# Weighing the values in pairs of units, up to two units behind the transposes, in a two-block attention kernel

## The chip, the cores and the metric

The kernel runs on one core of one Trainium2 chip. The metric is the device time of one execution in microseconds; the time given is the median of several executions.

## What is computed

Two blocks run one after the other on x of 2048 rows by 1024 columns, float32. The first has a gated short convolution and a "stick-breaking" attention. The second, in which the change lies, makes a projection of 2888 columns, a pooling mixer, and a sparse attention: an indexer of 8 heads scores all keys, the best 256 keys of each query are selected, and 8 heads (64 wide, 2 groups of keys and values) attend to the selected keys alone. Cut to what matters:

```python
def one_block(blk, qb, qib, wb):              # a block is 128 queries
    q_pos = blk * Q_BLOCK + jnp.arange(Q_BLOCK)
    logits = einsum('bqhd,bsd->bqhs', qib, k_idx) * IDX_DIM ** -0.5
    score = einsum('bqhs,bqh->bqs', relu(logits), wb) * N_IDX_HEADS ** -0.5
    score = where(key_pos[None, :] <= q_pos[:, None], score, -inf)
    _, sel = top_k(score, 256)
    s = einsum('bqhgd,bqkhd->bqhgk', qg, k[sel]) * HEAD_DIM ** -0.5
    p = softmax(where(sel <= q_pos, s, -inf))
    return einsum('bqhgk,bqkhd->bqhgd', p, v[sel])
```

The kernel does not gather. It computes the attention scores against all keys that are causal for the block, adds a bias of -1e30 to those that were not selected, and sums over all.

## The kernel before, in words

`phase_select_attend` is written as one program per engine, which meet at semaphores. The 16 blocks of 128 queries are taken in the order `ORDER` = 0, 1, 4, 6, 8, 10, 12, 14, 15, 13, 11, 9, 7, 5, 3, 2. Block number b of the sequence has `keys(b)` = 128 x (ORDER[b] + 1) keys, in groups of up to 512 (`parts`): 1, 1, 2, 2, 3, 3, 4, 4, 4, 4, 3, 3, 2, 2, 1 and 1 groups. A **slot** is a pair of heads ("sides" 0 and 1) of a block, four slots a block; a **unit** is one group of keys of one slot. There are 64 slots and 160 units, and as each block has four slots, every block begins with an even unit.

All engines walk over the units in step. For unit u:

- TensorE transposes the unit's exponentials of both sides (`turn_over`, L3167 to L3175; up to 4 transposes of 128 by 128 a side) into one of two PSUM banks `turn`, which it may only overwrite when ScalarE has copied the last contents out. It then makes the products of `share(u)` (`scores`, L3127 to L3154): products of the indexer for a block three ahead, and attention products for a slot some 1.6 slots ahead, each as two matmuls of up to 512 columns into one of five banks `pr`. Last it weighs (`weigh`, L3177 to L3190): per 128 keys and side one product of the probabilities with the values, 128 keys by 64 columns, added up in the single PSUM bank `o_ps` of the block. It is issued one unit behind. The trace records each such product as two matmuls, so a full unit has 16 records of L3188. In L3182 the first weighing of a block waits until ScalarE has copied `o_ps` of the block before.
- ScalarE copies the transposed exponentials of both sides to SBUF (`leave`, L2777), applies ReLU to the indexer's products (`rectify`, L2769), and computes the exponential of a whole row when its last attention product is masked (`raise_e`, L2760; up to 2048 wide). Then come the rarer steps: the copy of `o_ps` (`leave_outputs`, L2785), a sample, a square and four counts for the selection of the block two ahead.
- VectorE adds the bias to the attention products and finds their least value (`mask`, L2902), adds up the index scores (`add_score`, L2890), searches the threshold, and divides the copied outputs (`divide`, L3047).
- GpSimd does small steps of the search; SyncE loads queries, keys, values and the output weights and stores the outputs.

The work of a share is spread evenly by time (`timed`, L2432 to L2440). Probabilities have three buffers (`P_DEEP` = 3, L2383): `leave(u)` waits for the weighing of unit u - 3. `leave_outputs(qb - 1)` waits for the last weighing of block qb - 1. In the kernel before it stands at the end of the first unit of block qb in ScalarE's order:

```python
                qb = block_of(u)
                if first_step(u, 0) and qb:
                    leave_outputs(qb - 1)
```

and TensorE's order is, from L3192:

```python
            for u in range(-1, U):
                if u >= 0:
                    turn_over(u, 0)
                    turn_over(u, 1)
                for kind, qb, h, m in share(u):
                    scores(kind, qb, h, m)
                ...
                if u >= 1:
                    weigh(u - 1)
            weigh(U - 1)
```

Of the kernel before, what the change touches and what calls it, by code (L numbers as in the profile page):

```python
# [2358 lines left out]
def phase_select_attend(nc, sem, p_t, rot_hi, rot_lo, bit_int, bit_val, half_powers, rank_row, inverse_t, mix_t, ident, space, w_out):  # L2359
# [37 lines left out]
    def parts(qb):  # L2397
        return [(at, min(GROUP, keys(qb) - at)) for at in range(0, keys(qb), GROUP)]
# [5 lines left out]
    def groups_of(s):  # L2404
        return parts(s // PAIRS)
# [27 lines left out]
    for s in range(SLOTS):  # L2433
        qb, pair = divmod(s, PAIRS)
# [10 lines left out]
    U = len(units)  # L2445

    def share(u):

        if u < 0:
            return [p for at, p in timed if at < 0]  # L2450
        s, g = units[u]
        steps = len(groups_of(s))
        return [p for at, p in timed if at >= 0 and int(at) == s and int((at - s) * steps) == g]
# [18 lines left out]
    def first_step(u, pair):  # L2472
        return units[u][0] % PAIRS == pair and units[u][1] == 0

    def block_of(u):
        return units[u][0] // PAIRS
# [8 lines left out]
    def values_due(u, chunk):  # L2485

        return first_step(u, 1) and block_of(u) == max(0, first_with(chunk) - 2)
# [16 lines left out]
    with ExitStack() as ctx:  # L2504
# [252 lines left out]
        def _(act):  # L2757
            nc.scalar.preload_act_table_set("natural_log_exp_and_others")

            def raise_e(qb, h):  # L2760
                s, side = qb * PAIRS + h // 2, h % 2
                act.wait_ge(masked, masks[qb, h, len(parts(qb)) - 1] + 1)
                if qb >= 2:
                    act.wait_ge(inverted, qb - 1)
                row = arg[:, s % DEEP, side, 0:keys(qb)]
                nc.scalar.activation(row, row, ACT.Exp, scale=-1.0, bias=low_top[:, s % DEEP, side, len(parts(qb)) - 1:len(parts(qb))],  # L2766
                                     accum_out=total[:, qb % 2, h:h + 1]).then_inc(raised, 1)

            def rectify(qb, h, m):  # L2769
                n, half = parts(qb)[m][1], m % 2 * GROUP  # L2770
                p, a = number["index", qb, h, m], adds[qb, h, m // 2]
                act.wait_ge(product, p + 1)
                if a >= R_DEEP:
                    act.wait_ge(scored, a - R_DEEP + 1)
                nc.scalar.activation(relu[:, a % R_DEEP, half:half + n], pr[p % BANKS][:, 0:n], ACT.Relu).then_inc(relu_done, 1)  # L2775

            def leave(u, side):  # L2777
                s, g = units[u]
                w = groups_of(s)[g][1]
                act.wait_ge(turned, 2 * u + side + 1)  # L2780
                if u >= P_DEEP:
                    act.wait_ge(weighed, u - P_DEEP + 1)
                nc.scalar.activation(prob[:, u % P_DEEP, side, 0:w], turn[turn_of["prob", u, side] % 2][:, 0:w], ACT.Copy).then_inc(p_ready, 1)  # L2783
# [47 lines left out]
            def leave_values(chunk):  # L2831
                act.wait_ge(v_turned, chunk + 1)
                nc.scalar.activation(v_nat[:, 4 * chunk:4 * chunk + 4], turn[turn_of["values", chunk] % 2][:].rearrange("p (t d) -> p t d", d=P),
                                     ACT.Copy).then_inc(v_left, 1)
# [14 lines left out]
            for u in range(-1, U):  # L2849
                if u == 0:  # L2850
                    for j in range(2):
                        act.wait_ge(space.rows_out[j], 16 * space.rows_stored[j])
                    act.wait_ge(space.last_rows_out, 16)
                if u >= 0:
                    leave(u, 0)
                    leave(u, 1)
                for kind, qb, h, m in share(u):
                    if kind == "index":
                        rectify(qb, h, m)
                for kind, qb, h, m in share(u):  # L2860
                    if kind == "attend" and m == len(parts(qb)) - 1:
                        raise_e(qb, h)
                if u < 0:
                    leave_values(0)
                    continue
                qb = block_of(u)
                if first_step(u, 0) and qb:
                    leave_outputs(qb - 1)
                if units[u][1] == 0:
                    for k in weights_at.get(divmod(units[u][0], PAIRS), ()):  # L2870
                        split_weights(k)
                for chunk in range(1, CHUNKS):
                    if values_due(u, chunk):
                        leave_values(chunk)
                soon = to_select(u, 2)
                if in_quarter(u, 0, 0) and soon:
                    sample(soon)
                if in_quarter(u, 0, 2) and soon:
                    square(soon)
                for k, (pair, quarter) in enumerate(((1, 0), (1, 2), (2, 0), (2, 2))):  # L2880
                    if in_quarter(u, pair, quarter) and soon:
                        count_signs(soon, k)
                for t in range(2):
                    if first_step(u, 1 + t) and qb == LAST:
                        act.wait_ge(space.out_gated, t + 1)
                        nc.scalar.activation(space.out_m_hi[:, t], space.out_m[:, t], ACT.Copy).then_inc(space.out_m_hi_done, 1)
# [223 lines left out]
        def _(pe):  # L3110
# [66 lines left out]
            def weigh(u):  # L3177
                s, g = units[u]
                qb, pair = divmod(s, PAIRS)
                at, w = groups_of(s)[g]  # L3180
                kv = pair // (PAIRS // KV_HEADS)
                if pair == 0 and g == 0 and qb:  # L3182
                    pe.wait_ge(o_left, qb)
                pe.wait_ge(v_left, at // GROUP + 1)
                pe.wait_ge(p_ready, 2 * u + 2)
                for c in range(0, w, P):
                    for side in range(2):
                        ins = nc.tensor.matmul(o_ps[side * HD:side * HD + HD, pair * P:pair * P + P], v_nat[:, (at + c) // P, kv * HD:kv * HD + HD],  # L3188
                                               prob[:, u % P_DEEP, side, c:c + P], start=at + c == 0, stop=at + c + P == keys(qb))
                ins.then_inc(weighed, 1)  # L3190

            for u in range(-1, U):  # L3192
                if u >= 0:
                    turn_over(u, 0)
                    turn_over(u, 1)
                for kind, qb, h, m in share(u):
                    scores(kind, qb, h, m)
                if u < 0:
                    turn_values(0)
                if u >= 0:  # L3200
                    for chunk in range(1, CHUNKS):
                        if values_due(u, chunk):
                            turn_values(chunk)
                if u >= 1:
                    weigh(u - 1)
            weigh(U - 1)


# [239 lines left out]
```

## Time and profile before

| what | us |
|---|---|
| median of 3 runs (lowest, highest) | 3191.09 (3189.61, 3191.92) |
| span of the profiled execution | 3189.0 |
| TensorE busy (matmuls) | 2990.2 |
| VectorE busy | 2253.7 |
| ScalarE busy | 1624.1 |
| the selection and attention stage, in the span | 2312.2 to 2997.4 |

The span is the time from the first to the last instruction of one profiled execution; it stands 2.1 us below the median of the runs. Engines are PE (TensorE's matmuls), PEld (its weight loads, which overlap the matmuls), DVE (VectorE), ACT (ScalarE), POOL (GpSimd), SP (SyncE). Matmuls are pipelined, and their ends are modelled; their starts are the surer measure. A row of the timeline begins with the start and the time from there to the end, in microseconds; "x16" is a run of 16 like instructions; in brackets stands how long the engine was idle before it and what ended that.

### The profile page before, as it was taken

Reading aid. Unit: us, or ns where it says so; the run is one execution under the profiler, and the core shown is the slowest. Engines: PE = TensorE matmul, PEld = TensorE weight load, DVE = VectorE, ACT = ScalarE, POOL = GpSimd, SP = SyncE. Lnnn points to the kernel's source line nnn. Section 1 sums busy time; section 2 is a strip of 40 time slices with the busy share of each in tenths; the row PEclk is TensorE's granted clock in tenths of the full one; section 3 lists DMA queues with packets and bytes.
Section 4 is the critical chain, followed back from the end, with each engine's and each line's share of the span. In section 5 each row is a group of like instructions: output and inputs, shape, how many; then the busy total and the mean of one; then the engine's idle time right before and its main releaser. Section 6 shows DMA issues by size and latency. Waiting matters only on the chain. (4 is left out here: it accounts for less than half of the span.)

```text
span 3189.0 us, 48176 instructions
## 1 busy us (share of the span) xinstructions
PE 2990.2 (94%) x17460; PEld 2369.3 (74%) x17460; DVE 2253.7 (71%) x3296; ACT 1624.1 (51%) x2947; POOL 231.3 (7%) x519
## 2 busy tenths in 40 slices
PE   6999999999998999999999999999977889998899
PEld 5888788888777866677777777887756666776687
DVE  8888877753677758888878554524378989988543
ACT  5344422232545436777769423211288887887500
POOL 0000000000000001110100000000021321213100
PEclk8999999999999999999999999999989999999899
DMA  4434422244657432111136334232641111011665
GB/s 119 121 109 122 145 67 75 84 141 144 170 171 254 154 131 77 32 37 41 45 92 199 112 96 132 86 132 74 172 98 34 31 28 24 23 36 39 170 183 158
DMA packets 377860, 331.47 MB, mean 104 GB/s; under 512 B 100988, under 2 KB 331900, under 8 KB 371472
## 3 DMA queue, kind: packets, MB, share of 16 engines
q1 hardware_dynamic: 371784, 293.40, 32.4%
q0 software_dynamic: 5120, 34.67, 2.8%
q8 instruction: 142, 2.33, 0.3%
q14 instruction: 94, 0.77, 0.1%
q10 hardware_dynamic: 720, 0.31, 0.1%
HBM read 211.26 MB, written 107.10 MB: 100 GB/s over the span
## 5 line engine op out<-in xcount | busy, mean ns | idle before, releaser
L629 PE MATMUL p_oa_acc<-s_h_a_hi,s_mx_w_hi 128*128 128x512 f32 x768 | 301.8, 393 | 15.2 <-DVE s_h_a_lo L418 9.4
L323 ACT ACTIVATE s_mx_w_hi<-s_mx_raw 128x512 fp32r<-128x512 f32 x224 | 139.1, 629 | 320.6 <-PE p_oa_acc L629 256.8
L629 PE MATMUL p_oa_acc<-s_h_a_lo,s_mx_w_hi 128*128 128x512 f32 x768 | 300.4, 391 | 0.0
L629 PE MATMUL p_oa_acc<-s_h_a_hi,s_mx_w_lo 128*128 128x512 f32 x768 | 300.2, 391 | 0.0
L1598 DVE TENSOR_TENSOR_SCAN s_st_prod<-s_st_soft,s_st_prod 128x512 f32<-128x512 f32 x192 | 234.4, 1267 | 15.9 <-ACT s_st_soft L1525 15.9
L3174 PE MATMUL p_sa_turn<-s_ident,s_sa_arg 128*128 128x128 f32 x1088 | 166.3, 289 | 48.5 <-ACT s_sa_prob L2783 30.9
L1525 ACT ACTIVATE s_st_soft<-p_st_z 128x512 f32<-128x512 f32 (+3 forms) x320 | 153.7, 534 | 112.0 <-PE p_st_z L1650 112.0
L2345 PE MATMUL p_pr_ps<-s_h_hi,s_pr_w_hi 128*128 128x512 f32 (+1 forms) x712 | 195.4, 395 | 1.8 <-PEq L1712 1.2
L2766 ACT ACTIVATE s_sa_arg<-s_sa_arg,s_sa_low_top 128x128 f32<-128x128 f32 (+15 forms) x128 | 155.7, 1218 | 79.6 <-DVE s_sa_low_top L2918 79.6
L460 DVE TENSOR_TENSOR s_mx_w_lo<-s_mx_raw,s_mx_w_hi 128x512 fp32r<-128x512 f32 x224 | 153.5, 685 | 57.8 <-ACT s_mx_w_hi L323 56.3
L2345 PE MATMUL p_pr_ps<-s_h_lo,s_pr_w_hi 128*128 128x512 f32 (+1 forms) x712 | 191.5, 389 | 0.0
L2345 PE MATMUL p_pr_ps<-s_h_hi,s_pr_w_lo 128*128 128x512 f32 (+1 forms) x712 | 191.5, 389 | 0.0
L3174 PEld LDWEIGHTS p_sa_turn<-s_ident,s_sa_arg 128*128 128x128 f32 x1088 | 120.9, 145 | 86.4 <-issue 53.3
L2227 DVE TENSOR_TENSOR s_pr_w_lo<-s_pr_raw,s_pr_w_hi 128x1024 fp32r<-128x1024 f32 (+1 forms) x22 | 26.5, 1204 | 223.5 <-ACT s_pr_w_hi L2168 223.5
L629 PEld LDWEIGHTS p_oa_acc<-s_h_a_hi,s_mx_w_hi 128*128 128x128 f32 x768 | 145.0, 189 | 47.9 <-issue 17.9
L2775 ACT ACTIVATE s_sa_relu<-p_sa_pr 128x512 f32<-128x512 f32 (+3 forms) x304 | 155.5, 567 | 28.0 <-DVE s_sa_score L2899 13.8
L629 PEld LDWEIGHTS p_oa_acc<-s_h_a_hi,s_mx_w_lo 128*128 128x128 f32 x768 | 145.1, 189 | 30.4
L3188 PE MATMUL p_sa_o_sum<-s_sa_prob,s_sa_v_nat 128*64 128x128 f32 x2176 | 160.7, 288 | 7.4 <-ACT s_sa_o L2789 7.4
L629 PEld LDWEIGHTS p_oa_acc<-s_h_a_lo,s_mx_w_hi 128*128 128x128 f32 x768 | 145.2, 189 | 29.6
L2899 DVE SCALAR_TENSOR_TENSOR s_sa_score<-s_sa_relu,s_sa_w_idx,s_sa_score 128x1024 f32<-128x1024 f32 (+7 forms) x154 | 153.8, 1021 | 18.9 <-ACT s_sa_relu L2775 17.9
L3188 PEld LDWEIGHTS p_sa_o_sum<-s_sa_prob,s_sa_v_nat 128*64 128x64 f32 x2176 | 121.2, 141 | 58.9 <-issue 46.3
L2783 ACT ACTIVATE s_sa_prob<-p_sa_turn 128x512 f32<-128x512 f32 (+3 forms) x320 | 154.3, 541 | 11.2 <-PE p_sa_turn L3174 10.7
(379 smaller groups left out, 7408.7 us busy)
## 6 DMA issues: line engine op xcount, KB each, us to landing
s_mx_raw<-in_w_in_a SPq DMA_DIRECT2D x128, 256.0 KB, 3.8
s_pb_ada<-in_w_ada SPq DMA_DIRECT2D x16, 768.0 KB, 4.3
s_pr_raw<-in_w_in SPq DMA_DIRECT2D x21, 512.0 KB, 3.9
s_pr_work<-s_pr_stage SPq DMA_DIRECT2D x38, 256.0 KB, 4.2
d_rot_hi<-s_pr_rot POOLq DMA_DIRECT2D x9, 1024.0 KB, 4.3
d_rot_lo<-s_pr_stage POOLq DMA_DIRECT2D x9, 1024.0 KB, 6.2
d_y_t<-s_mx_y SPq DMA_DIRECT2D x16, 512.0 KB, 5.5
s_oa_y_raw<-d_y_t SPq DMA_DIRECT2D x16, 512.0 KB, 4.8
```

What stands on the lines that cost most here:

```text
L323: nc.scalar.activation(w_hi[:, m], raw[g % 2][:, m], ACT.Copy).then_inc(hi_done, 1)
L460: nc.vector.tensor_tensor(w_lo[:, m], raw[g % 2][:, m], w_hi[:, m].bitcast(F32), ALU.subtract).then_inc(lo_done, 1)
L629: ins = nc.tensor.matmul(bank, w[:, m, k, :], a[:, m, k, :], start=(k == 0 and n == 0), stop=(k == KH - 1 and n == 2))
L1525: nc.scalar.activation(soft[:, u % DEEP, s, 0:n], z[u % 2 * 2 + s][:, 0:n], ACT.Sigmoid, scale=-SCALE).then_inc(softened, 1)
L1598: nc.vector.tensor_tensor_scan(prod[:, b, s, 0:n][:, ::-1], back, back, carry, ALU.mult, ALU.bypass).then_inc(multiplied, 1)
L2345: ins = nc.tensor.matmul(ps[b % 2][0:cols, t * 512:(t + 1) * 512], w[b % 2][:, k, 0:cols], a[:, k, t * 512:(t + 1) * 512], start=(k == 0 a ...
L2766: nc.scalar.activation(row, row, ACT.Exp, scale=-1.0, bias=low_top[:, s % DEEP, side, len(parts(qb)) - 1:len(parts(qb))], accum_out=total[ ...
L2775: nc.scalar.activation(relu[:, a % R_DEEP, half:half + n], pr[p % BANKS][:, 0:n], ACT.Relu).then_inc(relu_done, 1)
L2783: nc.scalar.activation(prob[:, u % P_DEEP, side, 0:w], turn[turn_of["prob", u, side] % 2][:, 0:w], ACT.Copy).then_inc(p_ready, 1)
L2899: ins = nc.vector.scalar_tensor_tensor(s, relu[:, a % R_DEEP, 0:n], w, s, ALU.mult, ALU.add)
L3174: ins = nc.tensor.transpose(turn[i % 2][:, c:c + P], arg[:, s % DEEP, side, at + c:at + c + P], ident[:])
L3188: ins = nc.tensor.matmul(o_ps[side * HD:side * HD + HD, pair * P:pair * P + P], v_nat[:, (at + c) // P, kv * HD:kv * HD + HD], prob[:, u % ...
```

## The change

Even-numbered units are weighed a unit later, so that the weighings of an even unit and of the odd one behind it stand next to each other on TensorE: in its loop, an even u ends with the weighing of u - 2, and an odd u begins with the weighing of u - 2. The last two are weighed after the loop. ScalarE's copy of a block's outputs is put one unit later, at the end of the next block's second unit.

```diff
@@ -2864,7 +2864,7 @@
                     leave_values(0)
                     continue
                 qb = block_of(u)
-                if first_step(u, 0) and qb:
+                if u and first_step(u - 1, 0) and qb:
                     leave_outputs(qb - 1)
                 if units[u][1] == 0:
                     for k in weights_at.get(divmod(units[u][0], PAIRS), ()):
@@ -3190,6 +3190,8 @@
                 ins.then_inc(weighed, 1)
 
             for u in range(-1, U):
+                if u >= 2 and u % 2:
+                    weigh(u - 2)
                 if u >= 0:
                     turn_over(u, 0)
                     turn_over(u, 1)
@@ -3201,8 +3203,9 @@
                     for chunk in range(1, CHUNKS):
                         if values_due(u, chunk):
                             turn_values(chunk)
-                if u >= 1:
-                    weigh(u - 1)
+                if u >= 2 and u % 2 == 0:
+                    weigh(u - 2)
+            weigh(U - 2)
             weigh(U - 1)
```

## Rows read from the trace of the kernel before

**Rows 1.** The page's first line: the span.
```profile
span 3189.0 us, 48176 instructions
```

**Rows 2.** Windows: length, busy PE, PEld, DVE, ACT, POOL, clock, DMA share, GB/s; sums of five, of four.
```profile
2312.20:2997.40 685.20, 586.51 (x4486) 453.58 (x4486) 583.00 (x1233) 561.94 (x1122) 165.35 (x386) 0.95 0.21 48
...
2796.80:2821.00 24.20, 24.20 (x213) 18.85 (x211) 19.81 (x43) 20.94 (x37) 2.66 (x6) 1.00 0.13 24
...
sum 107.30, PE 107.16 PEld 84.89 DVE 89.97 ACT 94.99 POOL 9.76; mean PE 21.43 PEld 16.98 DVE 17.99 ACT 19.00 POOL 1.95
...
sum 68.90, PE 57.98 PEld 42.67 DVE 66.43 ACT 51.52 POOL 22.54; mean PE 14.50 PEld 10.67 DVE 16.61 ACT 12.88 POOL 5.64
```

**Rows 3.** Waits in the stage: engine, tile, line, releaser: us in total, times, longest.
```profile
PE p_sa_turn L3174 <- ACT s_sa_prob L2783: 30.9, 43, 2.1
...
PEld p_sa_turn L3174 <- issue: 53.3, 163, 2.3
PEld p_sa_o_sum L3188 <- issue: 46.3, 131, 0.7
```

**Rows 4.** Timeline of PE in the full stretch at 2796.8 to 2821.0.
```profile
2801.47 0.39 PE L3152 MATMUL p_sa_pr<-s_sa_k_hi,s_sa_ki_qi_q 128*128 128x512 f32 x1
2801.70 0.39 PE L3153 MATMUL p_sa_pr<-s_sa_k_lo,s_sa_ki_qi_q 128*128 128x512 f32 x1
2802.01 1.09 PE L3188 MATMUL p_sa_o_sum<-s_sa_prob,s_sa_v_nat 128*64 128x128 f32 x16
2803.04 1.09 PE L3174 MATMUL p_sa_turn<-s_ident,s_sa_arg 128*128 128x128 f32 x8
2803.89 0.48 PE L3152 MATMUL p_sa_pr<-s_sa_ki_qi_q 128*128 128x512 f32 x1
...
2810.97 0.66 PE L3188 MATMUL p_sa_o_sum<-s_sa_prob,s_sa_v_nat 128*64 128x128 f32 x8
2811.56 0.66 PE L3174 MATMUL p_sa_turn<-s_ident,s_sa_arg 128*128 128x128 f32 x4
```

**Rows 5.** Timeline of PEld at the stage's end.
```profile
2991.69 1.15 PEld L3188 LDWEIGHTS p_sa_o_sum<-s_sa_prob,s_sa_v_nat 128*64 128x64 f32 x12 [0.44 <-issue]
...
2994.64 2.17 PEld L3188 LDWEIGHTS p_sa_o_sum<-s_sa_prob,s_sa_v_nat 128*64 128x64 f32 x24 [0.33 <-issue]
```

**Rows 6.** Timeline of PE: transposes behind scores, in this stage and in the first block's attention.
```profile
2322.35 0.34 PE L3153 MATMUL p_sa_pr<-s_sa_ki_qi_q 128*128 128x384 f32 x1
2322.53 0.60 PE L3122 MATMUL p_sa_turn<-s_ident,s_sa_v_raw 128*128 128x128 f32 x4
...
1501.97 0.40 PE L1650 MATMUL p_st_z<-s_st_k_hi,s_st_q_lo 64*128 64x512 f32 x2
1502.30 0.88 PE L1668 MATMUL p_st_turn<-s_ident,s_st_prod 128*128 128x128 f32 x6
```

**Rows 7.** Timelines of ACT, PE and DVE at a block's start (2768.6).
```profile
2773.26 0.61 ACT L2789 ACTIVATE s_sa_o<-p_sa_o_sum 128x512 f32<-128x512 f32 x1
...
2777.89 1.79 ACT L2766 ACTIVATE s_sa_arg<-s_sa_arg,s_sa_low_top 128x1792 f32<-128x1792 f32 x1 [1.64 <-DVE s_sa_low_top L2918]
...
2779.68 1.06 ACT L2783 ACTIVATE s_sa_prob<-p_sa_turn 128x512 f32<-128x512 f32 x2
...
2778.45 0.40 PE L3153 MATMUL p_sa_pr<-s_sa_k_lo,s_sa_ki_qi_q 128*128 128x512 f32 x1
...
2780.40 0.90 PE L3174 MATMUL p_sa_turn<-s_ident,s_sa_arg 128*128 128x128 f32 x4 [0.53 <-ACT s_sa_prob L2783]
...
2782.08 0.39 PE L3153 MATMUL p_sa_pr<-s_sa_k_lo,s_sa_ki_qi_q 128*128 128x512 f32 x1
...
2783.13 0.69 DVE L2918 CUSTOM_DVE_ANT_0 s_sa_arg<-p_sa_pr,s_sa_bias 128x512 f32<-128x512 f32 x1
```

**Rows 8.** Windows around a fall of the clock; columns as in rows 2.
```profile
2928.00:2931.00 3.00, 1.07 (x17) 0.85 (x14) 1.71 (x7) 2.89 (x7) 0.69 (x2) 1.00 0.01 2
2931.00:2934.00 3.00, 3.00 (x17) 2.52 (x17) 1.64 (x5) 3.00 (x9) 0.69 (x2) 0.61 0.16 1
```

## The prediction

> **What bounds the kernel now.** I read three views. First the page and the busy times of stretches. The change touches only the selection and attention stage, 685.2 us of a 3189.0 us span [rows 1, 2]. In it, TensorE is busy for 586.5 of these, VectorE for 583.0, ScalarE for 561.9 [rows 2]: three engines at 82 to 86%, so the reader should expect the bound to change hands. It does, by the sums of two groups of stretches [rows 2]. Five stretches, 107.3 us together, have TensorE at 107.2, and in them VectorE has 17 us to spare. In the four stretches around the starts of the 4-group blocks VectorE has 66.4 of 68.9 us and TensorE only 58.0. Time saved on TensorE is worth its full price in the first kind and little in the second.
>
> Second, the waits [rows 3]: TensorE waits 30.9 us for probabilities to be copied out by ScalarE, in 43 places, so the turning and copying loop is tight. The weight loads stand idle 46.3 us before weighings and 53.3 us before transposes for nothing that the profile names ("issue"), 131 and 163 times. These small idles are what the change can remove.
>
> Third, the starts of matmuls in a full stretch [rows 4]. A 512-wide score matmul follows the last one after 0.23 us (2801.47, 2801.70); the weighing comes after 0.31, so entering it costs 0.08. A weighing of 16 records occupies 1.03 us until the transposes start (2802.01 to 3.04), one of 8 records 0.59 (2810.97 to 11.56): 0.055 a record and 0.15 fixed. So a weighing has 0.23 us around it that its own work does not need.
>
> **The change, part by part.** There are 160 units of work, and no instruction is added or dropped, only waits and places. Written out, TensorE's order was T S W T S W (transposes, scores, weighing) and becomes T S W W T S. Odd-numbered weighings stay where they were; each even-numbered one moves one unit later, next to its odd neighbour.
>
> Removed per pair of units: one entry S to W (0.08) and one W block's fixed part (0.15). Added: one seam W to W and one S to T. For W to W, the trace has one case, the two last weighings of the stage: 24 records in one run of loads of 2.17 us, with no idle, where 12 took 1.15 in the same slow state of the clock [rows 5]. The second twelve cost 1.02, less than a block by itself, so the seam is 0. For S to T, inside the stage the nearest case is a transpose of values behind a 384-wide score matmul: 0.18 us after it, which is its own 384/512 of 0.23 [rows 6]. That is 0. The farther case is the attention of the first block, where transposes start 0.33 us after a 512-wide score matmul of another tile (64 by 128): 0.10. I take 0, since the tile (128 by 128 on both sides) is the same as in the changed kernel; the other end leaves 0.13 of the 0.23. The saving is 0.23 x 79 pairs = 18.2 us if all of it counted.
>
> The rows tie these idles to a change of tile: 128 by 64 for the weighing, 128 by 128 for the rest. The Trainium skill, page TensorEngine Tiling (Array Packing), section Key Properties, says that changing the tiling mode drains TensorE; by it, S to T inside this stage would be free, as the nearer row has it, and the 0.10 of the farther one would be its own change of mode.
>
> How much counts? In the full stretches a pair takes 6 to 7 us (in [rows 4] a unit is about 3.0), so 107.3 us hold 16 pairs: 16 x 0.23 = 3.7 us, the low end. Of the other 63 pairs (14.5 us) I let a fifth count, 2.9, since there TensorE waits for others and a shorter weighing only lengthens the wait. Together -6.6 us, between -3.7 and -18.2.
>
> The move of the output copy. ScalarE's copy of a finished block's sums (0.61 us) goes from the block's first unit to its second. All blocks have a multiple of four units, so a block starts with an even unit, and its first weighing is now behind the scores of the third unit, in front of its partner. It needs the copy. In a 4-group block the second unit also holds an exponential, and the copy is queued behind it: in the block at 2768.6 the exponential runs 2777.89 to 2779.68, held until then by VectorE's mask [rows 7]. The copy then ends at 2780.3 and the weighing can start at 2780.4. TensorE finishes the third unit's scores at 2778.45 + 0.23 = 2778.7 now, and about a microsecond earlier with one weighing fewer ahead of it. Then two weighings of 1.03 and 0.87 and a seam follow, so the transposes of the fourth unit, which now start at 2780.40, start at 2782.4 to 2782.5: 2.0 to 2.1 us late. What is queued behind the waiting weighing is its partner, those transposes and the fourth unit's scores. Who waits for them is VectorE. Its mask of that unit's second attention product started at 2783.13, 0.81 us after the product was complete (2782.08 + 0.24), of which some 0.3 is passing on. So 0.5 us of the 2.1 is hidden and 1.5 is lost there, on the engine that bounds this stretch. There are four such boundaries. I take 1.5 less 0.3 that VectorE regains, 1.2 each: 4.8. The bounds are 0 (it regains all) and 4 x 2.1 = 8.4. By the code, the second unit of a 3-group block has no exponential at its end; in the 2-group and 1-group blocks it has one, but a narrower one, and TensorE waits there for other things anyway: 0, with the spare of the upper bound for them. The copy delays ScalarE's next copies of probabilities by 0.6 us as well, which is inside the same 2.1. In the full stretches between boundaries, nothing of this.
>
> Even transposes. Between the transposes of an odd unit and those of the next there were scores and a weighing; now only the scores, about 1.2 us. In that time ScalarE must copy side 0 (0.53 us, half of 1.06 [rows 7]). It does if it is free; where it is behind, TensorE stands where it used to weigh. The mean of the 43 present waits is 0.7 us. In every fifth or so of the full pairs I expect one of 0.4: +1.7, bounds 0 and 6. At waits that ScalarE causes anyway, before odd transposes, the second weighing fills the gap, so nothing is added there.
>
> The end. The last blocks are bound by the exponentials; two weighings instead of one stand before the last transposes: 12 more records at the low clock, 1.0 us [rows 5], of which 0.6 lands on the end. DMAs, SyncE's and GpSimd's queues are issued by the same steps as before; SyncE waits only for the division of the outputs, which has microseconds of room.
>
> Sum against the profiled execution's 3189.0 us: -6.6 + 4.8 + 1.7 + 0.6 = +0.5, so 3189.5. The median of the runs stands 2.1 us above that span (3191.09), which I add: 3191.6.
>
> **Rivals.** (B) The seams count nearly everywhere, because TensorE is in the loop even where it waits for ScalarE. For it: 30.9 us of waits in a loop through TensorE, and 160 units in which a seam delays the copies. Against it: VectorE's 66.4 of 68.9 us. Half of the 14.5 counting instead of a fifth, and the stalls at 2: -3.7 - 7.3 + 2 = -9, 3182. (C) The stall at a block's first weighing is paid in full on TensorE, and the even transposes wait in earnest: 8.4 + 4 + 0.6 against 3.7: +9.3, 3200. It is decided at the copy's end: if that is over 0.3 us behind the third unit's scores, (C) or the forecast holds; if ahead, (B). (D) The pause lets the clock fall. After 3 us with TensorE busy for 1.07 the granted clock was 0.61 in the next 3 [rows 8], which is half speed, 1.2 GHz, for part of them: 0.39 x 3 = 1.2 us each time. At four boundaries on top of (C): +14, 3205. [...] A page of the Trainium skill, TensorE: Matmul & The Clock Gate, Part 4, speaks against the change more strongly: transposes do not count as activity for the clock as matmuls do, and between the weighings there is now T S T S. By it the full pairs would run in part at 1.2 GHz; the full stretch at 2796.8 has 1.00 [rows 2] with transposes for 0.85 us (2803.04 to 2803.89) of each unit [rows 4], so the trace gives it little room. (E) The change does not do what it is meant to: whatever TensorE gains or loses is taken up by VectorE and ScalarE, 2 us to either side, inside the forecast.
>
> **How the numbers follow.** No change means within 0.2%, 6.4 us, about what a measurement of this kernel can tell. The forecast with (E): 0.43, within that bound. (B): 0.29, faster by more. (C): 0.20 and (D): 0.08, slower by more. The predicted time is the forecast's, 3191.6. The range runs from the middle of (B), 3181, to a little beyond (C), 3203; it leaves out 0.1 on either side. The forecast's own range is 3186 to 3197.
>
> **What would show it.** Right: "issue" idles before weighings fall from 131 to about 70 to 80 and before transposes by as many; runs of 32 weighing records in about 1.9 us; new waits of the weighing for ScalarE's copy of the outputs, about 2 us each, four times or more, each with VectorE idle behind it; the full stretches shorter by 0.23 a pair. Wrong: idles before transposes that follow scores (then the seam S to T costs), the waits for probabilities well over 31 us (then the even transposes decide), or a stage that is shorter by over 8 us.

## The result, and the profile after

| what | before | after |
|---|---|---|
| median of 4 runs each (lowest, highest), us | 3190.35 (3188.99, 3191.92) | 3210.68 (3209.24, 3211.04) |
| span of the profiled execution, us | 3189.0 | 3207.4 |
| selection and attention stage in it, us | 685.2 | 703.8 |

The ratio is 1.0064, 95% interval [1.0051, 1.0076]: slower by 0.64%, some 20 us, where 3191.6 was forecast, 0.5 us more than before. The time lies outside the range of 3181 to 3203. All of the loss is in the stage that was changed, 18.6 us by the two profiles.

The window of the stage after, with the columns of [rows 2]:

```profile
2312.50:3016.30 703.80, 580.62 (x4486) 466.87 (x4486) 583.59 (x1233) 563.66 (x1121) 158.32 (x386) 0.93 0.21 47
```

TensorE is busy 5.9 us less in it than in [rows 2] and the stage is 18.6 us longer: the seams did go, and TensorE waited more. Its clock is 0.93 where it was 0.95. Where it waits is in the groups of instructions of the stage. Before the bar stand busy time and mean ns, behind it the idle time just before the group and what ended it. The kernel before first, then after:

```profile
L3174 PE MATMUL p_sa_turn<-s_ident,s_sa_arg 128*128 128x128 f32 x1088 | 166.3, 289 | 48.5 <-ACT s_sa_prob L2783 30.9 <-ACT s_sa_arg L2766 10.4 <-ACT s_sa_v_nat L2833 6.3
L3188 PE MATMUL p_sa_o_sum<-s_sa_prob,s_sa_v_nat 128*64 128x128 f32 x2176 | 160.7, 288 | 7.4 <-ACT s_sa_o L2789 7.4
```

```profile
L3174 PE MATMUL p_sa_turn<-s_ident,s_sa_arg 128*128 128x128 f32 x1088 | 166.3, 290 | 61.6 <-ACT s_sa_prob L2783 43.5 <-ACT s_sa_arg L2766 12.2 <-ACT s_sa_v_nat L2833 5.0
L3188 PE MATMUL p_sa_o_sum<-s_sa_prob,s_sa_v_nat 128*64 128x128 f32 x2176 | 147.9, 290 | 9.1 <-ACT s_sa_o L2789 9.1
```

The weighings are busy for 12.8 us less, and the transposes wait for 13.1 us more. The waits in the stage (totals, times, longest) answer to [rows 3]:

```profile
PEld p_sa_turn L3174 <- issue: 69.2, 123, 3.5
...
PE p_sa_turn L3174 <- ACT s_sa_prob L2783: 43.5, 40, 3.1
...
PEld p_sa_o_sum L3188 <- issue: 22.4, 61, 0.7
...
PE p_sa_o_sum L3188 <- ACT s_sa_o L2789: 9.1, 7, 1.9
...
DVE s_sa_o L3051 <- ACT s_sa_o L2789: 3.1, 2, 1.6
```

The fourth of them, the weighing's wait for ScalarE's copy of the outputs, was in the kernel before:

```profile
PE p_sa_o_sum L3188 <- ACT s_sa_o L2789: 7.4, 6, 2.0
```

Of the idles before weighings 61 of 131 are left, where the prediction expected 70 to 80. Before transposes it expected as large a fall; there 123 of 163 are left, and their sum rose from 53.3 to 69.2 us. The waits for probabilities are no more numerous than before (40 for 43), but longer. Waits of the weighing for the copy are not new, as the prediction had it, but have moved: none of the 6 before was in a 4-group block, and now each of the four 4-group blocks has one, of 1.10, 1.77, 1.87 and 1.67 us (read from the trace's records). The last row is new: VectorE's division of the outputs, which the prediction gave "microseconds of room", now waits for the later copy.

**The full stretch.** TensorE's timeline, answering to [rows 4]:

```profile
2810.35 1.06 PE L3174 MATMUL p_sa_turn<-s_ident,s_sa_arg 128*128 128x128 f32 x8 [0.53 <-ACT s_sa_prob L2783]
...
2816.06 0.40 PE L3153 MATMUL p_sa_pr<-s_sa_k_lo,s_sa_ki_qi_q 128*128 128x512 f32 x1
2816.30 1.03 PE L3174 MATMUL p_sa_turn<-s_ident,s_sa_arg 128*128 128x128 f32 x8
...
2818.19 1.97 PE L3188 MATMUL p_sa_o_sum<-s_sa_prob,s_sa_v_nat 128*64 128x128 f32 x32
2820.09 0.66 PE L3174 MATMUL p_sa_turn<-s_ident,s_sa_arg 128*128 128x128 f32 x4
...
2833.37 1.04 PE L3174 MATMUL p_sa_turn<-s_ident,s_sa_arg 128*128 128x128 f32 x8
```

Transposes start 0.24 us after the last score matmul (2816.06, 2816.30), as a score matmul would: the seam S to T is 0. The 32 merged records take 1.90 us to the next transposes (2818.19 to 2820.09), where two blocks of 16 took 2 x 1.03 [rows 4]. From the first row to the last, which is four pairs of units, there are 23.02 us (2810.35 to 2833.37); in [rows 2] the same four pairs fill the window from 2796.80 to 2821.00, 24.2. That is 0.29 us a pair, a little more than the 0.23 forecast.

**A block's start.** After's timeline where the fourth unit of the block that starts at 2715.4 should be transposed, answering to [rows 7]:

```profile
2727.82 2.00 ACT L2766 ACTIVATE s_sa_arg<-s_sa_arg,s_sa_low_top 128x2048 f32<-128x2048 f32 x1 [1.79 <-DVE s_sa_low_top L2918]
...
2729.83 0.58 ACT L2789 ACTIVATE s_sa_o<-p_sa_o_sum 128x512 f32<-128x512 f32 x1
...
2730.45 3.43 PE L3188 MATMUL p_sa_o_sum<-s_sa_prob,s_sa_v_nat 128*64 128x128 f32 x32 [1.87 <-ACT s_sa_o L2789]
...
2733.81 1.25 PE L3174 MATMUL p_sa_turn<-s_ident,s_sa_arg 128*128 128x128 f32 x8
...
2736.02 0.75 DVE L2918 CUSTOM_DVE_ANT_0 s_sa_arg<-p_sa_pr,s_sa_bias,s_sa_low_top 128x512 f32<-128x512 f32 x1 [2.98 <-PE p_sa_pr L3153]
```

The copy stands behind the exponential, TensorE's weighing waits 1.87 us for it, and then the 32 records take 3.36 us to the transposes (2730.45 to 2733.81), not 1.9. The window around them has a granted clock of 0.55, where 0.5 is 1.2 GHz, so nearly all of it ran at that level:

```profile
2730.40:2733.90 3.50, 3.45 (x33) 3.12 (x34) 2.49 (x7) 3.44 (x8) 0.27 (x1) 0.55 0.00 0
```

VectorE then stands idle for 2.98 us. This is the forecast's stall and rival (D) on top of it. In the block of [rows 7] the same step is 3.1 us: the fourth unit's transposes are 3.9 us further behind those of before than the third unit's are, and an odd unit's are 0.8 behind in any case, for the second weighing now ahead of them. In the first two 4-group blocks the step is smaller, 1.8 and 1.5 us, and there the clock did not fall behind the wait.

### The profile page after: what moved, and what is told of

Read it like the earlier page. It is cut to its first block and busy times, and to the rows that moved or that the text cites. A ratio compares the mean times of both kernels' runs of the same rounds, so it can differ in the third digit from the quotient of the medians.

```text
span 3207.4 us, 48176 instructions
## 1 busy us (share of the span) xinstructions
PE 2985.4 (93%) x17460; PEld 2383.6 (74%) x17460; DVE 2254.0 (70%) x3296; ACT 1625.1 (51%) x2947; POOL 224.0 (7%) x519
## 5 line engine op out<-in xcount | busy, mean ns | idle before, releaser
L3174 PEld LDWEIGHTS p_sa_turn<-s_ident,s_sa_arg 128*128 128x128 f32 x1088 | 125.8, 147 | 103.1 <-issue 69.2
L2345 PEld LDWEIGHTS p_pr_ps<-s_h_hi,s_pr_w_hi 128*128 128x128 f32 (+1 forms) x712 | 132.0, 186 | 35.9 <-issue 5.9
L2918 DVE CUSTOM_DVE_ANT_0 s_sa_arg<-p_sa_pr,s_sa_bias,s_sa_low_top 128x512 f32<-128x512 f32 (+3 forms) x192 | 124.3, 647 | 46.5 <-PE p_sa_pr L3153 31.3
```

What stands on the lines that cost most here:

```text
L2345: ins = nc.tensor.matmul(ps[b % 2][0:cols, t * 512:(t + 1) * 512], w[b % 2][:, k, 0:cols], a[:, k, t * 512:(t + 1) * 512], start=(k == 0 a ...
L3174: ins = nc.tensor.transpose(turn[i % 2][:, c:c + P], arg[:, s % DEEP, side, at + c:at + c + P], ident[:])
```

## The experiments

All ratios are to the kernel before, run beside each kernel on the same chip. Its median there was between 3189.99 and 3191.48 us, so the ratios are to be compared and not the medians. "Copy" is ScalarE's copy of a block's outputs, and "the copy first" puts it at the head of the block's second unit, ahead of the copies of probabilities:

```diff
+                if u >= 1 and first_step(u - 1, 0) and block_of(u):
+                    leave_outputs(block_of(u) - 1)
                 if u >= 0:
                     leave(u, 0)
                     leave(u, 1)
...
-                if u and first_step(u - 1, 0) and qb:
-                    leave_outputs(qb - 1)
```

### Order and copy taken apart

e1_copy_first: after's order of weighings with the copy first. 

> The order of weighings as in the changed kernel; ScalarE copies a block's outputs at the head of the next block's second unit, ahead of the probabilities, and so ahead of the exponential. Theory A (the copy behind the exponential stalls TensorE at each block's first weighing, and the clock falls there): the stall at the fourth unit of the four 4-group blocks, 3 us each, goes, and with what is like it in the others 13 us or more come back: ratio to before about 1.001 to 1.002. Theory B (the pairing itself is the loss: the transposes of even units have only the scores as cover, their waits are longer and let the clock fall): little comes back, 1.004 to 1.006. Half-speed time in the stage by A about 75 us, by B over 85.

e2_old_copy: after's order with the copy where the kernel before has it. 

> The order of weighings as in the changed kernel, the copy of the outputs where the kernel before has it, at the end of the block's first unit. It now waits on ScalarE for two weighings instead of one, about 1 us more at each of 15 blocks, if ScalarE has nothing left to catch up. Theory A: 1.001 to 1.003, like the kernel with the copy first or 1 us behind it. Theory B: 1.004 to 1.006.

e3_copy_alone: before's order of weighings with after's place of the copy. 

> The order of weighings of before, the copy of the outputs one unit later, as in the changed kernel. TensorE then wants the copy at the end of the second unit, when the exponential has not even begun. Theory A: at least the 13 us of the changed kernel, since the wait is longer here: 1.005 or more. Theory B: 1.000 to 1.002.

e5_copy_first_alone: before's order with the copy first. 

> The order of weighings of before; only the copy of the outputs moves, to the head of the second unit. It shows whether that place has a price or a gain of its own, against which the kernels with pairs and the copy first are to be read. All theories: 0.999 to 1.001.

| kernel | median us | ratio [95%] | stage us |
|---|---|---|---|
| after | 3210.68 | 1.0064 [1.0051, 1.0076] | 703.8 |
| e1_copy_first | 3202.10 | 1.0040 [1.0026, 1.0054] | 694.0 |
| e2_old_copy | 3201.97 | 1.0035 [1.0021, 1.0048] | 694.0 |
| e3_copy_alone | 3245.01 | 1.0171 [1.0158, 1.0185] | 741.1 |
| e5_copy_first_alone | 3191.55 | 1.0006 [0.9997, 1.0015] | 683.6 |

The stage is counted from the first unit's transposes to the last weighing in one profiled execution. The windows of before and after (685.2 and 703.8) end 0.3 us later than that, so differences to them are good to 0.3 us.

The later copy costs 8 to 10 us of after's 20 (1.0064 less 1.0040 or 1.0035; stage 703.8 less 694.0), and it does not matter which of the earlier places it has. Without the later order it would be far dearer: in e3 the first weighing of a block comes a unit earlier and waits for the copy 15 times, 62.9 us in all. The order alone, in e1 and e2, still loses 11 to 13 us by the ratios and some 9 by the stage, though it removes seams. That the forecast did not have. e1 lies where theory B had it, e2 between the ranges of the two theories.

### Seams and cover

e4_unpaired takes e1 and pulls each pair apart. The late weighing of an even unit moves from behind the next even unit's scores to ahead of them, right behind the transposes; the odd one stays behind the scores. Even transposes still follow scores directly:

```diff
-                if u >= 2 and u % 2:
-                    weigh(u - 2)
                 if u >= 0:
                     turn_over(u, 0)
                     turn_over(u, 1)
+                if u >= 2 and u % 2 == 0:
+                    weigh(u - 2)
...
                 if u >= 2 and u % 2 == 0:
-                    weigh(u - 2)
+                    weigh(u - 1)
```

> Transposes, one weighing, scores, one weighing in even units; transposes and scores alone in odd ones; the copy first. Each weighing has its two seams again, but between odd and even transposes there are only scores, as in the changed kernel. Against the kernel with the copy first it costs the seams alone: 0.3 us in each pair of the full stretches, some 5 us in all (Theory A and B alike): ratio 0.0015 above that one. If seams count everywhere, 20 us above it. The full stretches themselves should be as long as before.

It took 3213.60 us, 1.0073 [1.0059, 1.0086], with a stage of 705.7. So e1 is 11.7 us shorter than e4 (705.7 less 694.0), more than twice the 5 us that were expected, and e4 is 20.5 longer than before (705.7 less 685.2). These are not the prices of the seams and of the bare transposes alone. In e4 the scores of every even unit stand behind a weighing, as they do neither in e1 nor before, and VectorE's waits for score products are longer. Before, e1 and e4:

```profile
DVE s_sa_arg L2918 <- PE p_sa_pr L3153: 50.0, 58, 3.6
```

```profile
DVE s_sa_arg L2918 <- PE p_sa_pr L3153: 60.7, 65, 4.7
```

```profile
DVE s_sa_arg L2918 <- PE p_sa_pr L3153: 80.8, 73, 4.8
```

How much of the 11.7 is seams and how much the later scores was not measured. e1 itself is free of that question: 9 us more than before in the stage, with all that its pairs save already taken off. The groups of the transposes of e1 and e4 in the stage show where TensorE waits:

```profile
L3174 PE MATMUL p_sa_turn<-s_ident,s_sa_arg 128*128 128x128 f32 x1088 | 165.3, 289 | 69.1 <-ACT s_sa_prob L2783 51.4 <-ACT s_sa_arg L2766 11.6 <-ACT s_sa_v_nat L2833 5.6
```

```profile
L3174 PE MATMUL p_sa_turn<-s_ident,s_sa_arg 128*128 128x128 f32 x1088 | 165.6, 289 | 72.7 <-ACT s_sa_prob L2783 52.8 <-ACT s_sa_arg L2766 11.3 <-ACT s_sa_v_nat L2833 7.3
```

48.5 us of idle before transposes have become 69.1 and 72.7. I sorted these idles, where over 0.3 us before a unit's first transpose, by the unit's parity and the groups of its block (us; counted from the trace's records):

| kernel | even: 1, 2, 3, 4 groups | sum | odd: 1, 2, 3, 4 groups | sum |
|---|---|---|---|---|
| before | 1.2, 3.9, 7.3, 1.2 | 13.6 | 0, 5.7, 2.7, 7.6 | 16.0 |
| after | 1.7, 12.4, 20.3, 4.0 | 38.3 | 0, 2.3, 1.6, 0 | 3.9 |
| e1_copy_first | 2.1, 12.0, 22.2, 8.9 | 45.3 | 0, 3.0, 1.8, 0 | 4.8 |
| e4_unpaired | 2.6, 14.1, 20.7, 7.6 | 44.9 | 0, 0.6, 2.2, 3.8 | 6.6 |
| e9_other_parity | 0.9, 3.4, 4.0, 0 | 8.3 | 1.1, 7.0, 7.1, 15.4 | 30.6 |

Even transposes, which in e1 lost the weighing in front of them, wait 32 us more than before; odd ones, which have two in front of them, 11 less.

Not every idle is a loss. How much longer than before the blocks are, from a block's first transposes to those of the next, again from one profile each (us, summed over the blocks of so many groups):

| kernel | 1 group | 2 groups | 3 groups | 4 groups |
|---|---|---|---|---|
| after | -1.0 | 2.8 | 10.8 | 6.1 |
| e1_copy_first | -3.1 | 2.2 | 10.6 | -0.6 |
| e4_unpaired | -2.6 | 4.3 | 15.1 | 4.1 |
| e5_copy_first_alone | -2.5 | 0.6 | 0.0 | 0.6 |
| e9_other_parity | -1.8 | 2.2 | 3.6 | 0.2 |
| e13_lag_two_one_divide | -0.7 | 4.9 | 3.3 | 3.1 |

The row of e5, whose stage should be as before, shows how far one profile can be trusted. e1's loss is in the 3-group blocks. There its idle, even and odd together, rose by 14.0 us; in the 2-group blocks it rose by 5.4 and the time by 2.2; in the 4-group blocks the odd transposes gave back what the even ones took, 7.6 for 7.7, and the time is as before. (e13 is a kernel of the last part below.)

One case of the loss is TensorE in a 3-group block. The kernel before:

```profile
2892.24 1.09 PE L3188 MATMUL p_sa_o_sum<-s_sa_prob,s_sa_v_nat 128*64 128x128 f32 x16
2895.18 0.89 PE L3174 MATMUL p_sa_turn<-s_ident,s_sa_arg 128*128 128x128 f32 x4 [1.85 <-ACT s_sa_prob L2783]
...
2896.61 0.39 PE L3153 MATMUL p_sa_pr<-s_sa_k_lo,s_sa_ki_qi_q 128*128 128x512 f32 x1
2896.93 1.09 PE L3188 MATMUL p_sa_o_sum<-s_sa_prob,s_sa_v_nat 128*64 128x128 f32 x16
2897.96 1.09 PE L3174 MATMUL p_sa_turn<-s_ident,s_sa_arg 128*128 128x128 f32 x8
```

And e1:

```profile
2899.12 1.15 PE L3174 MATMUL p_sa_turn<-s_ident,s_sa_arg 128*128 128x128 f32 x4 [3.15 <-ACT s_sa_prob L2783]
...
2901.34 0.63 PE L3153 MATMUL p_sa_pr<-s_sa_k_lo,s_sa_ki_qi_q 128*128 128x512 f32 x1
2901.90 3.50 PE L3188 MATMUL p_sa_o_sum<-s_sa_prob,s_sa_v_nat 128*64 128x128 f32 x32
2905.34 0.87 PE L3174 MATMUL p_sa_turn<-s_ident,s_sa_arg 128*128 128x128 f32 x6
```

ScalarE is held in both by an exponential of 1.36 us and a count of 0.92 behind it. Before, a weighing of 1 us lies inside the wait and costs nothing, and 1.85 us are left idle. In e1 the whole wait is bare, 3.15 us; the weighing is done afterwards, on the path; and from late in this idle on the clock is at 1.2 GHz (the window below has 0.54), so that the score matmuls follow each other after 0.42 us instead of 0.23 and the 32 records take 3.44, where after has 1.90 for them at full clock. From these transposes to the next it is 6.22 us where it was 2.78. Of the 3.44 us lost in this one unit, 0.87 is the weighing made afterwards, at full clock (1.90 less 1.03), and 2.57 is the clock. The whole block is 5.8 us longer than before. The window of e1 around it:

```profile
2898.00:2905.40 7.40, 6.28 (x41) 5.10 (x42) 1.54 (x4) 4.83 (x11) 1.38 (x4) 0.54 0.07 4
```

### Where pairs cost, and where not

e6_pair_in_four and e8_pair_by_slot have the copy first and pair only where I expected the waits to be before the odd transposes. Between them and e11 only the condition differs:

```diff
+            pending = []
+
+            def defers(u):
+                return u % 2 == 1 and len(groups_of(units[u][0])) == 4
...
-                if u >= 1:
-                    weigh(u - 1)
+                if u >= 1:
+                    pending.append(u - 1)
+                    while pending and not defers(u):
+                        weigh(pending.pop(0))
```

> Pairs of weighings in the six or so hundred keys and more of the 4-group blocks alone, single weighings elsewhere, the copy first. Theory B1 (the loss of pairing sits in the 3-group blocks, where TensorE waits at an even unit's transposes with no weighing left in front of them, and where the clock then falls): the 10 us that those blocks lost come back, 0.997 to 1.0005. Rival B2 (pairing costs wherever it is, by bunching the products for VectorE): a loss remains, 1.001 or more, in the 4-group blocks.

e8 also pairs in 3-group blocks, ahead of the third unit of every slot but the first. 

> As pairs in the 4-group blocks, and in the 3-group blocks a pair in front of the third unit of each slot but the first, where TensorE waits most, so that it is the second unit's transposes that have only scores as cover. B1: those waits hide two weighings now; 0.001 below the kernel with pairs in the 4-group blocks alone. B2: 0.001 or more above it.

e11_pair_not_in_three pairs everywhere but in the 3-group blocks (`!= 3`). It leaves out the last weighing but one of the stage, at most 1 us (12 records at the low clock [rows 5]). 

> After's order with the copy first, but in the blocks of three groups each weighing is issued one unit behind, as before. Theory (the 3-group blocks hold most of the loss of the order, some 10 us of it): 1.000 to 1.002. Rival (the loss is spread, or lies in the blocks of one and two groups): 1.0025 to 1.004.

e12_pair_in_four_old_copy is e6 with the copy at before's place. 

> Pairs only in the blocks of four groups, and the copy of the outputs where the kernel before has it, at the end of the first unit. Theory (the 0.23 to 0.30 us of a pair count in the full stretches, and the copy at its old place costs nothing): 16 to 32 pairs, -3 to -5 us, 0.9985 to 0.9992. Rival (VectorE and ScalarE take the gain up): 0.9995 to 1.0005.

e9_other_parity pairs everywhere, but ahead of even transposes, so that the odd ones are bare, and carries no weighing over a block's start: `return u % 2 == 0 and not first_step(u, 0)`. 

> Pairs everywhere as in the changed kernel, but of the other parity: each odd unit ends with the weighings of u - 2 and u - 1 (before even transposes), an even unit that is not the first of its block ends with none; no weighing is kept over a block's start, and the copy of the outputs stands at the head of the second unit. Theory (a weighing that used to fill TensorE's wait for ScalarE's copies is missing from half of the waits, and has to be made afterwards): the same number of pairs and of uncovered transposes, now the odd ones; slower than before by the order of the kernel with after's order and the copy first, 1.002 to 1.005, the loss again in the blocks of three groups. Rival (it is the one weighing that is carried over a block's start that costs, together with the lag): 0.997 to 1.001.

| kernel | median us | ratio [95%] |
|---|---|---|
| e6_pair_in_four | 3192.15 | 1.0004 [0.9995, 1.0014] |
| e8_pair_by_slot | 3190.77 | 0.9997 [0.9988, 1.0007] |
| e12_pair_in_four_old_copy | 3190.10 | 1.0005 [0.9996, 1.0014] |
| e11_pair_not_in_three | 3195.27 | 1.0017 [1.0008, 1.0026] |
| e9_other_parity | 3197.18 | 1.0024 [1.0015, 1.0034] |

Leaving the 3-group blocks alone takes e1's 1.0040 down to 1.0017, leaving the 1- and 2-group blocks alone as well takes it to 1.0004 (the intervals of these two overlap a little). That fits the two tables. e11 and e9 were run on another chip than e1 and e6, each beside its own kernel before. e9 shows that it is not after's parity: with the other one the bare transposes are the odd ones, they now hold 30.6 us of idle, and the kernel is slower again. Where its loss arises is open. Its theory had it in the 3-group blocks, which are 3.6 us longer in its profile with 1.1 us more idle before transposes. The 4-group blocks have 6.6 us more idle and are 0.2 longer. None of these beats the kernel before, and e8's 0.0007 below e6 is inside the intervals. e12 was expected at 0.9985 to 0.9992 and missed that: pairs in the full stretches alone bring nothing that the medians show, although the four blocks together are 2.3 us shorter in its profile and e6's than in before's (237.2 for 239.5). In these blocks the idle only changed sides: in e6 8.4 us before even transposes and none before odd ones, where before had 1.2 and 7.6.

### Two units behind without pairs

If the missing cover were all, a kernel that weighs every unit two units behind, unpaired, each weighing still between scores and transposes, should lose nothing. The last weighing of a block is then issued behind the scores of the next block's second unit, and its copy stands at the head of the third:

```diff
-                if u >= 1:
-                    weigh(u - 1)
+                if u >= 2:
+                    weigh(u - 2)
+            weigh(U - 2)
             weigh(U - 1)
```

> Every weighing two units behind its transposes, none paired, each at its unit's end: a weighing stands in front of all transposes as before. The copy comes at the head of the third unit. B1: the lag by itself costs nothing, 1.000 to 1.002, with little more half-speed time than before (72 us in the stage). Rival B3 (the longer lag is what costs, through the buffers of the probabilities or the later outputs): 1.004 or more.

It took 3210.22 us, 1.0059 [1.0046, 1.0072], a miss for B1 and in the range of its rival B3. VectorE's timeline in the second block shows one part of it:

```profile
2358.92 0.69 DVE L3051 TENSOR_TENSOR s_sa_o<-s_sa_o,s_sa_spread 128x512 f32<-128x512 f32 x1 [5.28 <-ACT s_sa_o L2789]
```

The division stands in the block's second slot, which in a 1-group block is the second unit, ahead of the copy. e10_lag_two_divide_later moves it one slot later everywhere, e13_lag_two_one_divide only in this block.

> All weighings two units behind, none paired, the copy at the head of the third unit, as in the earlier run of that order, and VectorE's division one slot later. Theory D (of that run's loss, 5.6 us at one boundary are VectorE's wait of 5.28 us in the division for the late copy, and more of it at other boundaries): 1.003 to 1.005 against 1.0059, no wait of the division for the copy. Rival (that wait only took the place of others): 1.0055 to 1.006.

> All weighings two units behind, none paired, the copy at the head of the third unit; VectorE's division is one slot later in the first block that has one, and in its old place in all others, the last ones too. Theory F (a weighing two units behind costs nothing as long as each unit has one between its scores and the next transposes; what the two earlier runs of this order lost was the division's wait for the late copy in the second block, 5.3 us, and in the second of them the later division in the last blocks, 6.8 us behind a DMA): 1.000 to 1.003. Rival G (the longer lag costs by itself, 10 us and more): 1.0035 to 1.005.

e10: 3202.45 us, 1.0039 [1.0025, 1.0052]. The wait for the copy is gone, but near the end of the stage the moved division waits for a transfer:

```profile
2983.90 0.69 DVE L3051 TENSOR_TENSOR s_sa_o<-s_sa_o,s_sa_spread 128x512 f32<-128x512 f32 x1 [6.82 <-DMA s_sa_spread<-d_inverse_t]
```

e13, without these two waits, still took 3202.61 us, 1.0034 [1.0024, 1.0044]. That is outside theory F's range, and 0.0001 short of rival G's. Its profile shows a part of the rest at the blocks' starts: the weighings wait 12.8 us for the copy in 9 places, where they waited 7.4 in 6 before, and the four 4-group blocks, of whose loss nearly all arises there, are 3.1 us longer of 10.5 in the stage. There ScalarE does the exponential, the copy and only then the probabilities, and the block's first weighing waits:

```profile
2784.05 1.79 ACT L2766 ACTIVATE s_sa_arg<-s_sa_arg,s_sa_low_top 128x1792 f32<-128x1792 f32 x1 [1.65 <-DVE s_sa_low_top L2918]
...
2785.84 0.58 ACT L2789 ACTIVATE s_sa_o<-p_sa_o_sum 128x512 f32<-128x512 f32 x1
...
2786.47 1.09 PE L3188 MATMUL p_sa_o_sum<-s_sa_prob,s_sa_v_nat 128*64 128x128 f32 x16 [1.47 <-ACT s_sa_o L2789]
2787.49 0.66 PE L3174 MATMUL p_sa_turn<-s_ident,s_sa_arg 128*128 128x128 f32 x4
```

In the kernel before a weighing ran under the exponential there, and TensorE was idle for 0.53 us only [rows 7]. A weighing two units behind has, at the third unit, nothing to weigh but a block whose bank is still full. So part of the order's loss goes with the cover that is missing by parity, and a part of the price of a longer lag arises at the blocks' starts. The rest of e13's loss is open. The three buffers of probabilities are not it: neither in e13 nor in after, e1 or e7 do the waits of the stage have one of ScalarE's copies of probabilities for a weighing. Whether an earlier place of the copy in ScalarE's order would spare e13 the stall was not tried. How the 11 to 13 us of after's order divide between parity and lag was not measured; the other-parity kernel, which carries nothing over a block's start, lost 7.7 us of 3190.

## Why the prediction was wrong

**Seams: right for each pair, open in the sum.** 0.23 us a pair was forecast and 0.29 measured in the full stretch. The seam S to T is 0 and so is W to W. By the Trainium skill, TensorEngine Tiling (Array Packing), Key Properties, a change of tiling mode drains TensorE, and S to T, which changes none, would be free; the trace agrees, with 0.24 us from the last score matmul to the transposes. How many pairs count was not measured cleanly. -6.6 was forecast, between -3.7 and -18.2. e1 is 11.7 us shorter than e4, but that holds e4's later scores too. In e6 and e12, which pair the 4-group blocks alone, these four blocks are 2.3 us shorter than before for 32 pairs, and the medians show nothing. So the low end of 3.7, the full price in the full stretches, is not confirmed either.

**The even transposes: the step that failed.** The text took "in every fifth or so of the full pairs ... one of 0.4: +1.7, bounds 0 and 6". (A fifth of its 16 full pairs at 0.4 would be 1.3; the sum hardly feels it.) Measured: 20.6 us more idle before transposes in e1 (69.1 for 48.5), and e1, whose copy is not late, is 9 us longer in the stage after all that its pairs save. With the forecast's terms for seams and even transposes it should have been 4.9 us shorter. So the term is some 9 us plus what the seams give: 15 with the forecast's 6.6, and 20.5 by e4, later scores included. Each is beyond the upper bound of 6. It was also priced in the wrong place. Of the 45.3 us before even transposes in e1, 34.2 lie in the 2- and 3-group blocks and 8.9 in the 4-group blocks, where all but two of the 16 full pairs lie, and 10.6 us of the longer time are in the 3-group blocks. The price was worked out for a ScalarE that is free, or nearly so, and needs 0.53 us to copy a side. But TensorE's long waits stand where ScalarE is busy with other work (1.36 and 0.92 us in the case at 2895.18), and there the weighing in front of the transposes was filling the wait. Taken away it is done behind the wait, on the path. The prediction saw half of it, that at odd transposes "the second weighing fills the gap", and did not write down the mirror image, what the gap before even transposes loses. The 30.9 us in [rows 3] are what was left idle behind that filling, not the length of the waits. That it is the missing cover and not the longer lag is shown for single places and argued for the sum. e13, with the longer lag and without bare transposes, lost as much as e1, but elsewhere: 3.3 us of it in the 3-group blocks, where e1 lost 10.6.

**The copy: right mechanism, too small.** +4.8 was forecast, bounds 0 and 8.4; it measured 8 to 10. In the 4-group blocks after is 6.7 us longer than e1 (6.1 against -0.6). The steps at their fourth units, 1.8, 1.5, 3.3 and 3.1 us, add up to 9.7, so some 3 us of them were regained, where the forecast had 2.1 at each and 0.9 of it hidden or regained. The two long ones are those where the clock fell. The rest of the cost, some 3 us, is outside the 4-group blocks, where the forecast had put 0.

**The clock.** Rival (D) had a chance of 0.08 and happened in part. Time at 1.2 GHz in the stage, by the trace's clock records, was 71.7 us before, 95.6 after, 85.3 in e1 and 71.7 in e6. 24 us more at half speed are worth up to 12 us, an estimate from these times; they are contained in the losses above. The other warning, from the Trainium skill, TensorE: Matmul & The Clock Gate, Part 4, was that transposes do not count as activity as matmuls do. It did not show itself: a full stretch of after, with T S T between its paired weighings, kept 1.00.

```profile
2797.00:2833.00 36.00, 34.86 (x317) 28.45 (x315) 31.57 (x64) 31.85 (x56) 5.79 (x15) 1.00 0.19 38
```

**The end** (+0.6) was too small to be told apart.

**The rivals.** (C) named both places that failed, at 8.4 and 4 us; the first was about right, the second is 15 to 20 by the readings above. (C) with (D) gave 3205, nearest to the 3210.68 measured. By the stages of the profiles the steps are +20.5 from before to e4 (bare transposes, lag, later scores), -11.7 from e4 to e1 (pairs, and the scores early again) and +9.8 from e1 to after (the copy), where the forecast had +1.7, -6.6 and +4.8. The steps that need no e4 are +8.8 and +9.8.

## What to carry to other kernels

An instruction that stands in front of its engine's wait is free work as long as it fits in the wait; moving it elsewhere can cost its full length, as at 2895.18, even if the move saves something of its own. So before reordering, list the waits together with what runs just ahead of them, and price each move at the waits, not in the full stretches. An idle that grows is not yet a loss, as e9's 4-group blocks show; look whether the block around it grew. And what is put behind a long instruction on another engine (here a 0.6 us copy behind an exponential of 2 us) is late by what is left of it.

## What was not expected of the hardware

The clock fell to 1.2 GHz around single idles of TensorE of 1.87 us (0.55 in the window at 2730.4) and 3.15 us (0.54 in the one at 2898.0) in otherwise busy stretches, but not behind the 1.85 us at 2895.18 in the kernel before. The length of the idle alone does not tell it. Two of after's waits for the copy, with like work behind them:

```profile
2666.98 1.97 PE L3188 MATMUL p_sa_o_sum<-s_sa_prob,s_sa_v_nat 128*64 128x128 f32 x32 [1.77 <-ACT s_sa_o L2789]
```

```profile
2791.57 3.12 PE L3188 MATMUL p_sa_o_sum<-s_sa_prob,s_sa_v_nat 128*64 128x128 f32 x32 [1.67 <-ACT s_sa_o L2789]
```

The granted clock over these two weighings:

```profile
2666.98:2670.00 3.02, 3.02 (x40) 2.81 (x41) 2.84 (x8) 3.02 (x5) 0.00 (x0) 1.00 0.00 0
```

```profile
2791.57:2794.62 3.05, 3.05 (x32) 2.72 (x32) 2.13 (x6) 3.02 (x6) 0.09 (x1) 0.60 0.00 0
```

The longer idle left the clock whole, and its 32 records took 1.90 us to the next transposes; behind the shorter one they took 3.05. Where the clock fell, it could cost more than the work it fell on: 2.57 us beside the 0.87 of the late weighing at 2901.90. The fixed 0.15 us of a weighing block and its 0.08 of entry are not all that a pair saves: 0.29 instead of 0.23.
